# A state recurrence rewritten: the inverse's factors applied to the right side in PSUM, twin products in one bank, one hand-written order for two directions

## The reference, cut to what matters

```python
def wkv7_scan(S0, inputs, reverse):
    def step(S, inp):
        r, w, k, v, kk, a = inp
        S = (S * w[:, :, None, :]
             - jnp.einsum('bhvk,bhk->bhv', S, kk)[..., None] * (kk * a)[:, :, None, :]
             + v[..., None] * k[:, :, None, :])
        return S, jnp.einsum('bhvk,bhk->bhv', S, r)
    S, y = lax.scan(step, S0, xs, reverse=reverse)

S_cf, y_cf = wkv7_scan(S0, dir_inputs(f_ctx, 0), reverse=False)
S_cb, y_cb = wkv7_scan(S0, dir_inputs(f_ctx, 1), reverse=True)
_, y_lf = wkv7_scan(S_cf, dir_inputs(f_lat, 0), reverse=False)
_, y_lb = wkv7_scan(S_cb, dir_inputs(f_lat, 1), reverse=True)
```

## Time and profile before

| | before |
|---|---|
| median of 3 runs | 3787.6 us (3785.87 to 3789.56) |
| the profiled execution | 3791.85 us, span 3790.0 us, mean granted clock 0.968 |
| PE / PEld busy | 3543.5 / 2969.8 us (93% / 78%) |
| DVE / ACT / POOL busy | 2157.8 / 1416.4 / 145.1 us (57% / 37% / 4%) |
| chain that ended last | PE 76%, DVE 14%, DMA 5%, ACT 4%, issue 2% |
| DMA | 453.90 MB, mean 120 GB/s |

### The profile page before, as it was taken

The page is one execution under the profiler, slowest core; times in us unless marked ns, Lnnn a source line. Parts: engine busy times, 40 slices in busy tenths (PEclk is TensorE's granted clock), DMA queues, the critical chain, the costliest instruction groups (busy, mean ns, idle before and its releaser), DMA issues.

```text
span 3790.0 us, 61710 instructions
## 1 busy us (share of the span) xinstructions
PE 3543.5 (93%) x26870; PEld 2969.8 (78%) x26870; DVE 2157.8 (57%) x3440; ACT 1416.4 (37%) x2310; POOL 145.1 (4%) x258
## 2 busy tenths in 40 slices
PE   6999999888799999999987999999999999999898
PEld 4887885778778878877875998767887778879898
DVE  3765445777756763567466554653464443566675
ACT  3222334444332222322245543443242332445553
POOL 0110000000000100010100000020000000010000
PEclk8999998899999999999998999999999999999999
DMA  6664120000025652465624552221224552223453
GB/s 221 210 196 138 52 91 28 3 3 3 3 78 178 200 161 95 162 217 187 137 96 154 158 186 82 67 73 61 89 89 167 179 176 100 82 91 129 153 182 112
DMA packets 268413, 453.90 MB, mean 120 GB/s; under 512 B 15376, under 2 KB 158864, under 8 KB 262896
## 3 DMA queue, kind: packets, MB, share of 16 engines
q1 hardware_dynamic: 241296, 357.79, 28.8%
q0 software_dynamic: 26848, 92.17, 8.2%
HBM read 447.24 MB, written 1.94 MB: 119 GB/s over the span
## 4 chain that ended last, share of the span: by engine, by line
PE 76%; DVE 14%; DMA 5%; ACT 4%; issue 2%; SPq 0%; DVEq 0%; ACTq 0%
PE bank L1129 75%; DVE W L1957 4%; DVE W L1948 3%; DVE WR L1948 2%; ACT W L1603 2%; ACT WR L1603 1%; DMA ring<-in_w_ada 1%; PE bank L1374 1%; DMA ring<-in_w_up 1%; DMA ring<-in_w_mod 1%; DVE H L1948 1%; DVE HL L1948 1%; DMA ring<-in_ffn_out 1%; DVE small L2265 0%; ACT H L1603 0%
## 5 line engine op out<-in xcount | busy, mean ns | idle before, releaser
L1129 PE MATMUL bank<-HH,WR 128*128 128x512 f32 (+1 forms) x9312 | 2440.2, 349 | 79.1 <-DVE WR L1948 49.2
L1129 PEld LDWEIGHTS bank<-HH,WR 128*128 128x128 f32 x9312 | 1648.2, 193 | 333.8 <-DVE WR L1948 62.7
L1129 PE MATMUL bank<-HL,WR 128*128 128x512 f32 (+1 forms) x4656 | 1606.1, 345 | 0.0
L1948 DVE TENSOR_TENSOR WR<-ring,WR 128x2048 fp32r<-128x2048 f32 (+3 forms) x300 | 673.4, 2249 | 533.6 <-ACT WR L1603 533.0
L1129 PEld LDWEIGHTS bank<-HL,WR 128*128 128x128 f32 x4656 | 898.6, 193 | 96.9
L1603 ACT ACTIVATE WR<-ring 128x2048 fp32r<-128x2048 f32 (+3 forms) x300 | 561.8, 1879 | 820.3 <-PE bank L1129 621.6
L1603 ACT ACTIVATE W<-bank 64x256 f32<-64x256 f32 (+3 forms) x676 | 294.0, 444 | 789.1 <-PE bank L1129 745.0
L1129 PE MATMUL bank<-W 64*64 64x64 f32 (+5 forms) x6304 | 351.6, 249 | 50.0 <-ACT W L1603 29.1
L1957 DVE SCALAR_TENSOR_TENSOR W<-ring,vec,W 128x1024 f32<-128x1024 f32 x252 | 311.6, 1280 | 89.6 <-DMA ring<-in_w_mod 66.0
L1129 PEld LDWEIGHTS bank<-W 64*64 64x64 f32 (+3 forms) x6304 | 266.1, 141 | 121.6 <-ACT W L1603 48.9
L1957 DVE SCALAR_TENSOR_TENSOR W<-bank,vec,W 128x510 f32<-128x510 f32 (+1 forms) x206 | 130.5, 634 | 186.5 <-ACT W L1603 182.9
(11 more groups left out here) (114 smaller groups left out, 2215.0 us busy)
## 6 DMA issues: line engine op xcount, KB each, us to landing
ring<-in_ffn_in SPq DMA_DIRECT2D x176, 512.0 KB, 5.1
ring<-in_w_mod POOLq DMA_DIRECT2D x128, 512.0 KB, 4.5
ring<-in_w_in SPq DMA_DIRECT2D x52, 1024.0 KB, 5.1
ring<-in_ffn_out SPq DMA_DIRECT2D x176, 256.0 KB, 3.6
ring<-in_w_up SPq DMA_DIRECT2D x88, 512.0 KB, 5.0
ring<-in_w_ada SPq DMA_DIRECT2D x32, 1024.0 KB, 5.7
ring<-in_w_down SPq DMA_DIRECT2D x88, 256.0 KB, 3.5
ring<-in_w_ada POOLq DMA_DIRECT2D x32, 512.0 KB, 4.6
```

The source lines that it names most:

```text
L1129: return e.matmul(o, l, r, start=start, stop=stop, skip_group_check=True)
L1948: put(e.tensor_tensor(o, a, b, op), *events)
```

## The change

`rwkv` no longer advances generators. One list, `WKV_TURN`, says for a turn in which order the 140 steps of both directions come. A step is written `name/dl` or `name.h/dl`: capitals and `dec` are products on PE, small letters are what ACT or DVE does with a result, h is the half, d the direction, and l is 0 for chunk c and 1 for chunk c - 1: a turn holds the first part of one chunk and the second part of the chunk before. `WKV_ROWS` and `WKV_ALONE` say which engine does a step (a for ACT, v for DVE, one letter for each half). Nine turns cover eight chunks.

The matrices `inv` and `w1t` are no longer formed. The right side (Z = al S + aak v) is multiplied by the factors of the inverse one after the other: W = q2 Z, then U1, U2 and U add to the same bank (`start=False`), V uses its upper half. Two products that are needed together (N with its transpose, KB, AR, M) lie in the lower and upper half of one bank and are masked or copied by one instruction of 512 columns for each half of the partitions. Banks are handed out as four fixed pairs by `wkv_pairs`, in the order of the list. The state has two tiles in turn, S0 and S1. The transpose of v is kept for the other direction and made only in chunks with c % 4 < 2. The removed functions are those printed above; of the new ones:

```diff
-        ROUNDS = 29
+        WKV_TURN = (
+            "AR/01 Q3/11 Z/01 srho/11 q2.0/01 z.1/01 q2.1/11 q2.0/11 dec/00 z.0/01 ar.1/01 M/01 ebe/00 M/11 "
+            "eal/00 ar.0/01 epi/00 epz/00 ska/00 W/01 m.0/01 m.0/11 m.1/01 W/11 m.1/11 w.1/01 w.0/01 M2/01 M2/11 "
+            "w.0/11 U1/01 w.1/11 mm.0/01 mm.1/01 sbe/00 ua.1/01 U1/11 mm.1/11 ua.0/01 ua.1/11 mm.0/11 dec/10 "
+            "sal/00 AR/11 eal/10 U2/01 epz/10 ua.0/11 sal/10 U2/11 epi/10 ar.1/11 ebe/10 ska/10 ar.0/11 ub.1/01 "
+            "ub.0/01 ub.1/11 N/00 sbe/10 ub.0/11 V/01 v.1/01 nn.1/00 to.1/00 V/11 N/10 nn.0/00 v.0/01 U/01 "
+            "to.0/00 v.0/11 v.1/11 U/11 KB/00 q0/00 u.0/01 u.1/01 u.0/11 u.1/11 N2/00 to.1/10 n2.1/00 Y/01 "
+            "n2.0/00 nn.0/10 to.0/10 nn.1/10 SS/01 y.1/01 y.0/01 Q1/00 kb.1/00 SS/11 s.1/01 s.0/01 VT/10 q1.1/00 "
+            "kb.0/00 q1.0/00 s.0/11 vt.1/10 N2/10 s.1/11 Y/11 AAK/10 sm/11 vt.0/10 q0/10 n2.1/10 n2.0/10 y.1/11 "
+            "y.0/11 Q2/00 aa.0/10 KB/10 x.1/00 x.0/00 VT/00 aa.1/10 srho/00 Q1/10 q1.1/10 kb.0/10 vt.0/00 vt.1/00 "
+            "q1.0/10 Z/10 AAK/00 kb.1/10 Q2/10 z.0/10 z.1/10 sm/01 Q3/00 x.0/10 aa.0/00 aa.1/00 q2.1/00 x.1/10 ").split()
+        WKV_ALONE = dict.fromkeys(("ebe", "eal", "epz", "epi"), "a") | dict.fromkeys(("ska", "sbe", "sal", "srho", "q0", "sm"), "v")
+        WKV_ROWS = {"kb": "aa", "vt": "aa", "n2": "aa", "x": "aa", "m": "av", "mm": "va", "z": "aa", "w": "va", "ua": "va", "ub": "aa", "v": "aa", "u": "va", "nn": "vv", "to": "vv", "aa": "vv", "ar": "vv", "q1": "vv", "q2": "vv", "s": "vv"}
+        WKV_LEFT = {"dec": ("ebe", "eal", "epz", "epi"), "N": ("nn", "to"), "KB": ("kb",), "VT": ("vt",), "AAK": ("aa",), "AR": ("ar",),
+                    "N2": ("n2",), "Q1": ("q1",), "Q2": ("x",), "Q3": ("q2",), "M": ("m",), "M2": ("mm",), "Z": ("z",), "W": ("u",),
+                    "Y": ("y",), "SS": ("s",)}
+        WKV_PAIR = {}
...
+        def wkv_pairs(steps_):
+            group = {y: x for x in WKV_LEFT for y in WKV_LEFT[x]}
+            left = {x: sum(1 if y in WKV_ALONE else 2 for y in WKV_LEFT[x]) for x in WKV_LEFT}
+            free, seen = [(i, None) for i in range(4)], collections.Counter()
+            for _, name, h, who, c, d in steps_:
+                if name in WKV_LEFT:
+                    WKV_PAIR[name, c, d] = free.pop(0)
+                elif name in group:
+                    x = group[name]
+                    seen[x, c, d] += 1
+                    if seen[x, c, d] == left[x]:
+                        free.append((WKV_PAIR[x, c, d][0], (x, c, d)))
...
             barrier()
             ORDER.append(("wkv_start",))
-            ORDER.extend(("wkv", d) for d in range(2))
-            for c in range(8):
-                for r in range(1, ROUNDS + 1):
-                    ORDER.extend(("wkv", d) for d in range(2))
+            steps_ = wkv_steps()
+            wkv_pairs(steps_)
+            ORDER.extend(steps_)
...
+            def opened(name, c, d):
+                i, before = WKV_PAIR[name, c, d]
+                if before is not None:
+                    for x in WKV_LEFT[before[0]]:
+                        if x in WKV_ALONE:
+                            q.wait_ge(ACTS, (x, *before[1:]))
+                        else:
+                            left(x, *before[1:])
+                return banks[2 * i:2 * i + 2]
+            def w_n(c, d):
+                q.wait_ge(DVES, ("sal", c, d))
+                q.wait_ge(DVES, ("sbe", c, d))
+                o = opened("N", c, d)
+                times(o, d, 256 * d, (T["al"].at, T["be"].at))
+                made(times(o, d, 256 - 256 * d, (T["be"].at, T["al"].at)), "N", c, d)
+            def w_z(c, d):
+                q.wait_ge(DVES, ("sal", c, d))
+                left("aa", c, d)
+                S, v = old_state(c, d), vt(c, d)
+                o = opened("Z", c, d)
+                made(times(o, d, 0, (T["al"].at, S), (T["aak"].at, v)), "Z", c, d)
+            def w_w(c, d):
+                left("q2", c, d)
+                left("z", c, d)
+                made(times(opened("W", c, d), d, 0, (T["jd"].at, T["z"].at), start=True), "W", c, d)
+            def w_u1(c, d):
+                left("m", c, d)
+                left("w", c, d)
+                made(times(chain(c, d), d, 0, (one("ab", 1), T["w"].at), start=False), "U1", c, d)
+            def w_v(c, d):
+                left("ub", c, d)
+                made(times(chain(c, d), d, 256, (T["n2"].at, T["w"].at), start=False), "V", c, d)
+            def w_u(c, d):
+                left("v", c, d)
+                made(times(chain(c, d), d, 0, (T["n2"].at, T["z"].at), start=False), "U", c, d)
+            def w_y(c, d):
+                left("ar", c, d)
+                left("u", c, d)
+                S, v = old_state(c, d), vt(c, d)
+                o = opened("Y", c, d)
+                made(times(o, d, 0, (S, T["rho"].at), (v, one("ar", 1)), (T["u"].at, one("ar", 0))), "Y", c, d)
...
+            def copied(event, dst, name, at, w, c, d, h):
+                q.wait_ge(MM, (name, c, d))
+                i = result(name, at, w, c, d, h)
+                act(dst, i.rearrange("p (i c) -> p i c", i=2) if w == 512 else i, ACT.Copy, (event, c, d, h))
+            def e_ub(c, d, h):
+                q.wait_ge(MM, ("U1", c, d))
+                copied("ub", T["w"].half(d, h), "U2", 0, 256, c, d, h)
...
+            def e_nn(c, d, h):
+                q.wait_ge(MM, ("N", c, d))
+                if c:
+                    q.wait_ge(MM, ("M2", c - 1, d))
+                    q.wait_ge(MM, ("U1", c - 1, d))
+                tt(T["ab"].part(d, h), blocks(result("N", 0, 512, c, d, h)), mask("dlow", h, 2, 2), ALU.mult, ("nn", c, d, h))
+            def e_s(c, d, h):
+                q.wait_ge(MM, ("SS", c, d))
+                q.wait_ge(DVES, ("S", c - 1, d))
+                if c:
+                    q.wait_ge(MM, ("Z", c - 1, d))
+                    q.wait_ge(MM, ("Y", c - 1, d))
+                tt(T[f"S{c % 2}"].half(d, h), result("SS", 0, 256, c, d, h), T[f"S{(c - 1) % 2}"].half(d, h), ALU.add, ("s", c, d, h))
```

More of the change, by code:

```diff
@@ new lines, in times, with made @@
+            def times(o, d, at, *terms, start=None):
+                for s in range(4):
+                    for h in range(2):
+                        for i, (l, r) in enumerate(terms):
+                            first = i == 0 if start is None else start and s == 0
+                            x = mm(o[h][64 * h:64 * h + 64, at + 64 * s:at + 64 * s + 64], l(4 * d + s, h), r(4 * d + s, h),
+                                   first, i == len(terms) - 1)
+                return x
+            def made(x, name, c, d):
+                x.then_inc(MM.sem, MM.mark((name, c, d)))
@@ new lines, in w_dec @@
+            def w_dec(c, d):
+                off = WKV_OFF[d][c]
+                i, hf = off // P, (off // 64) % 2
+                dec = opened("dec", c, d)[0][:, :].rearrange("p (s a c) -> p s a c", s=4, a=2)
+                t0 = CST[("trif", "trib")[d]][0]
+                tri = cst[:, t0:t0 + 256].rearrange("p (a c) -> p a c", a=2)[:, :, 64 * hf:64 * hf + 64]
+                for s in range(4):
+                    x = mm(dec[:, s, :, :], LT[:, d, i, s * P:(s + 1) * P], tri, True, True)
+                made(x, "dec", c, d)
@@ new lines, in w_vt, with w_aak, w_ar @@
+            def w_vt(c, d):
+                off = WKV_OFF[d][c]
+                o = opened("VT", c, d)
+                made(times(o, d, 0, (lambda s, h: F[64 * h:64 * h + 64, 8 + s % 4, off:off + 64], eye)), "VT", c, d)
+            def w_aak(c, d):
+                q.wait_ge(DVES, ("ska", c, d))
+                q.wait_ge(DVES, ("sal", c, d))
+                made(times(opened("AAK", c, d), d, 0, (T["ka"].at, T["al"].at)), "AAK", c, d)
+            def w_ar(c, d):
+                q.wait_ge(DVES, ("sbe", c, d))
+                q.wait_ge(DVES, ("ska", c, d))
+                q.wait_ge(DVES, ("srho", c, d))
+                o = opened("AR", c, d)
+                times(o, d, 0, (T["be"].at, T["rho"].at))
+                made(times(o, d, 256, (T["ka"].at, T["rho"].at)), "AR", c, d)
@@ new lines, in e_kb, with e_vt @@
+            def e_kb(c, d, h):
+                if c:
+                    q.wait_ge(MM, ("SS", c - 1, d))
+                copied("kb", T["kb"].half(d, h), "KB", 0, 512, c, d, h)
+            def e_vt(c, d, h):
+                if c > 3:
+                    for z in ("Z", "Y", "SS"):
+                        q.wait_ge(MM, (z, c - 4, d))
+                        q.wait_ge(MM, (z, 4 * (c // 4) - 1 - c % 4, 1 - d))
+                copied("vt", T["vt"].place(*divmod(3 - c % 4 if d else c % 4, 2), h), "VT", 0, 256, c, d, h)
@@ new lines, in e_sm @@
+            def e_sm(c, d, h):
+                q.wait_ge(DVES, ("s", c, d, 0))
+                q.wait_ge(DVES, ("s", c, d, 1))
+                q.wait_ge(ACTS, ("epz", c, d))
+                S = every(T[f"S{c % 2}"], d)
```

(3 more changed lines are left out.)

588 lines of the change are left out of this document (263 added, 325 removed).

## The result

The changed kernel takes 3654.6 us (median of 4 runs, 3643.1 to 3659.2) beside 3786.7 for the kernel before on the same chip: ratio 0.9644, 95% interval 0.9626 to 0.9662. The profiled execution took 3651.1, its span is 3649.2. The forecast was 3673, so the change saved some 18 us more than that.

The account below looks back on a forecast made before the run. The recurrence, 358.4 us, was taken as unhidden, with PE needing 33.2 of 44.4 us a turn. Seven turns of 30.0 plus ends 15.6 and 18.3 make 243.9, 114.5 less: 3673 us, range 3653 to 3712.

Parts of the forecast that it names:

- Where the time goes: Recurrence, 358.4 us without DMA traffic: nothing hides behind it, so what is saved there is saved whole.
- PE work: TensorE in a turn: 53 blocks at 0.49 us plus 2.0 for decays, 27.9 us, 5.3 less than before.
- DVE and ACT: Other engines in a turn: DVE 25.0 us against 34.3 busy before; ACT 18.7 us, as now, never the bound.
- The tight place: KB/00 takes N/00's bank pair 2.9 us after it; N's four masks need 2.6, plus sbe/10 queued on DVE.
- The turn: Recurrence, one turn: 30.0 us, between PE alone at 27.9 and 39.1 with all of today's loss.
- The ends: First and last of nine turns, each only partly filled: 15.6 and 18.3 us, walked with the listed durations.
- The low end of the range: Whole kernel at 3653 us: turns at PE's own 27.9 with shorter ends, 223 us, saving 135; chance 0.05.
- the upper end: Top of the forecast range, whole kernel at 3712 us: turn 35.5, ends 36.
- The cause of the gain: Gaps in the old turn: opened by the 30 or so copies and masks that DVE loses; 11.2 us lost per turn.
- Turns that don't overlap: Rival, recurrence: a chunk's two parts run one behind the other, 33.9 each, 271 us, saving 87: 3700; chance 0.15.
- waits that stay: Rival, recurrence: only work leaves, waits for pairs replace the 11.2 us loss, saving 47: 3741; chance 0.08.
- The slower one: Rival, recurrence: half clock over most of the stretch from PE's short gaps, 83 us slower: 3871; chance 0.02.

Follow-up runs that it names:

- the ten extra blocks: Changed kernel with five one-block products per direction and chunk (AAK, N2, Q1, Q2, M2) computed twice into the same bank: 3698.1 us, ratio 0.9759.
- the stagger alone in the old kernel: Kernel before with only the order of rounds changed, direction 1 running 14 rounds behind direction 0: 3776.7 us, ratio 0.9966.
- relief of DVE: Kernel before, direction 1 fourteen rounds behind, and the eleven copies per direction shared by DVE and ACT all given to ACT: 3809.6 us, ratio 1.0048.
- the run made for it: Changed kernel with chunk c's second-part steps all behind those of its first, so turns do not overlap: 3686.3 us, ratio 0.9734.
- The run with bursts on DVE: Changed kernel with the sum that makes jd computed 10 more times in a row, per direction and chunk: 3736.7 us, ratio 0.9859.
- ten more instructions a turn: Changed kernel with five more DVE instructions per direction and chunk: repeating jd's sum in a row, 3678.5 us; at five places, 3669.0 us.

## Why the prediction was right and wrong

- **Where the time goes** (the recurrence, nothing outside it): right. The recurrence is 132.8 us shorter; what else differs is within the spread.
- **PE work** (53 blocks, 27.9 a turn): the count is right, 851 and 883 records against 848 and 16 of decays in the mean. The rate was a little high: a turn of 27.87 less 2.18 for the decays is 25.7 for 54 blocks, 0.476 us each or 29.7 ns a record, where the working had 30.5; the ten extra blocks gave 0.468 to 0.486. With that PE's need is 27.4.
- **DVE and ACT**: right to within a microsecond or two. 51 and 55 instructions, 22.4 and 24.0 us, where the working had 52 and 25.0; ACT 42 to 50 and 15.9 to 18.7, for 18.7. Wide masks took 689 ns in the mean for 0.72, and the four masks of N 2.08 together for 2.34. The 0.36 of a whole-height instruction stands on no row (two took 0.76); alone they took 0.42 here.
- **The tight place** (KB/00 behind N/00): it is tight, and holds by 0.17 us. In the timelines of PE and DVE after:

```profile
732.81 1.10 PE L1200 MATMUL bank<-H 64*64 64x64 f32 x32
...
736.57 1.12 PE L1200 MATMUL bank<-cst,H 64*64 64x64 f32 x32
```

```profile
734.32 2.08 DVE L2081 TENSOR_TENSOR W<-bank,cst 64x512 f32<-64x512 f32 x4
```

  The last mask ends at 736.40 and KB starts at 736.57.
- **The turn: here the prediction failed.** The step took "30.0: some seven of 40 products wait a typical 0.3 us", a habit of the kernel before. Measured: no wait at all, 27.4 us. The working had compared the steps' distances with their needs and found all but one larger, and that one level (2.9 against 2.6 and a scaling); by it next to nothing should wait, and the 2.1 us above PE's 27.9 were an allowance without a row of this list behind it. Sized: 7 x (30.0 - 27.4) = 18.2 us, all but 0.1 of the 18.3 by which the saving was too small. Of it 7 x 2.1 = 14.7 are the waits, and 7 x 0.5 = 3.5 the rate. (The ends, 0.3 longer than forecast, and the start, read 0.4 too late, nearly cancel.)
- **The low end of the range** was PE's need at the too high rate, with ends of 27.9; its own sum gives 3652, where the range says 3653 (and the terms of the upper end, 35.5 and 36, give 3714 for 3712). In the recurrence its two terms missed in opposite ways: the turns were 0.5 us shorter each (3.5 in all), which "PE alone" didn't allow for, since the rate came from one row; the ends were 226.0 - 7 x 27.4 = 34.2 us, 6.3 longer than 27.9, and in sum what the walk gave (15.6 + 18.3 = 33.9). So the recurrence, 226.0, stayed above the 223 of the low end. That the time as a whole reached the edge came with the few microseconds outside the recurrence, which are spread; there the range had no room for them.
- **The cause of the gain** was only half right. Per turn, 44.4 to 27.4 us: 5.2 are blocks that are gone (11 at 0.476); 2.7 came with the stagger alone in the old kernel, the clock's dip among them; the other 9.1 are gaps that neither stagger nor relief of DVE closed in the old kernel. Of these 4.1 hang on the overlap of turns in the new list, and 5.0 are left. These parts were each measured with the rest in one state and need not add up. What closes the 5.0, shorter product-copy chains of the new arithmetic or the order of the list within a chunk, wasn't told apart and stays open: the old arithmetic has no such list, and the new one with both directions at the same step wasn't run.
- **The rivals.** Turns that don't overlap, and waits that stay: neither happened, and the first costs about what its case said: 30 us more in the run made for it, 27 in the working (271 for 243.9). The slower one, half clock through frequent small waits: did not happen, since there are none. The granted clock was 1.00 in all full turns, at 40 products through four pairs of banks. By the rule that the Trainium skill states (TensorE: Matmul & The Clock Gate, A second HAM failure mode: psum-queue depth-cycling) the clock swings where a kernel goes round through its PSUM banks with small idles between groups of products. This trace goes round through the banks but has no such idles, and no swing. The run with bursts on DVE, with waits of 4.0 us and a clock of 0.91, shows that the clock itself was there to be lost. The run with transposes and products in turn lost it too, 0.50 for 44 us, with next to no wait in PE's list.

## What to carry to other kernels

When an order is written out by hand, walk it: if every product's distance to its input is at least that input's chain of latencies, take the engine's own time as the forecast and not a share of the old waits, and reserve doubt for the rate, checked at more than one row. Two streams side by side at the same step leave their gaps together, but moving them apart alone was worth 2.7 us of 17.0 here: the chain of each was longer than the other stream could fill. In a fixed order an engine's slack is that of one place, not of its sum: ten more instructions a turn cost 28 us in two bursts and 16 spread. And a list of waits shows only idle time: a delay shorter than the record before it is seen in the starts alone.

## What the hardware did that was not expected

- Going from ordinary products to transposes and back on TensorE costs about 0.26 us a round, by the starts of both runs; the recurrence took 66 us more when they alternate, some 49 of it in the pairs themselves, and 19 when in fours. The Trainium skill (Perfetto Trace Analysis, Transposes) recommends the transpose instruction over a standard matmul for logical transposes. For 64x64 f32 tiles among other products the runs here show the opposite: 3718 and 3681 us against 3656 with identity products.
- The granted clock fell to 0.50 behind transposes and products in turn although PE's list has no wait there (706 to 900). So a list free of waits doesn't by itself keep the clock; how densely records follow each other differed too. Which of the two, the kind of instruction or the sparser records, is not shown.
- The decays' product did not change its time when it contracted over 64 rows instead of 128: 1.16 us for eight records, and 226.3 and 226.4 us for the recurrence.
- With no gaps and a clock of 1.00, 64x64 f32 products run at 29.7 ns a record over whole turns, in a list whose blocks wait for semaphores of the other engines.
